# Grouped attention in a two-layer backbone: inverse sums spread by transfers through DRAM, and the bias table built one stage earlier

## What is computed

```
h = rms_norm(x, norm_g) * (1 + scale) + shift          # 1280 tokens, latent and context
q, k, v, g = split(h @ w_in)                           # 8 heads of q, 2 of k and v, 128 wide; g is 1024 wide
q, k = rope(rms_norm(q, q_g)), rope(rms_norm(k, k_g))  # rope on the latent tokens alone
s = q @ k.T * 128 ** -0.5                              # latent q: 1280 keys; context q: 256 keys
o = softmax(s) @ v                                     # = (exp(s - max) @ v) / sum(exp(s - max))
y = (o * silu(g)) @ w_out
```

## Time and profile before

| | |
|---|---|
| median of 3 runs | 1547.32 us (1546.25 to 1550.59) |
| profiled execution | 1546.84 us, its span 1545.1 us |
| TensorE | 1495.9 us busy, 97% of the span |
| VectorE | 1003.6 us, 65% |
| ScalarE | 811.1 us, 52% |
| GpSimd | 419.4 us, 27% |
| DMA | 252.23 MB; SP's queue 51.5% of 16 engines' span |
| mean granted TensorE clock | 0.988 |

### The profile page before, as it was taken

The page is one execution under the profiler, slowest core; times in us unless marked ns, Lnnn a source line. Parts: engine busy times, 40 slices in busy tenths (PEclk is TensorE's granted clock), DMA queues, the critical chain, the costliest instruction groups (busy, mean ns, idle before and its releaser), DMA issues. The chain is left out here.

```text
span 1545.1 us, 26314 instructions
## 1 busy us (share of the span) xinstructions
PE 1495.9 (97%) x9467; PEld 1310.5 (85%) x9467; DVE 1003.6 (65%) x2139; ACT 811.1 (52%) x1848; POOL 419.4 (27%) x513
## 2 busy tenths in 40 slices
PE   6999999999999999989999999999998999999998
PEld 3788788897898898978888888889997889899996
DVE  5665645428888888864348966576221887787883
ACT  7422321128777777754554333444111887777772
POOL 2322101002222111100012333221390454554541
PEclk9899999999999999999999999999998999999999
DMA  9435425409111244023224454478957999999882
GB/s 358 161 122 157 129 83 178 159 18 274 24 25 24 81 157 143 7 88 116 82 89 127 131 166 139 132 219 268 288 142 216 301 297 272 257 264 274 260 232 68
DMA packets 195653, 252.23 MB, mean 163 GB/s; under 512 B 32978, under 2 KB 157476, under 8 KB 195492
## 3 DMA queue, kind: packets, MB, share of 16 engines
q1 hardware_dynamic: 193076, 242.16, 51.5%
q10 hardware_dynamic: 2448, 8.39, 1.9%
HBM read 187.59 MB, written 78.76 MB: 172 GB/s over the span
## 5 line engine op out<-in xcount | busy, mean ns | idle before, releaser
L1195 ACT ACTIVATE prob<-S,nm,qk_inv 128x512 f32<-128x512 f32 (+1 forms) x208 | 146.3, 707 | 3.5 <-DVE nm L1131 3.5
L600 PE MATMUL pp<-h_hi,w_hi 128*128 128x512 f32 (+1 forms) x408 | 147.6, 362 | 0.0
L2593 DVE CUSTOM_DVE_ANT_0 nprob<-nS,bias_set 128x640 f32<-128x640 f32 x128 | 105.0, 821 | 61.6 <-PE nS L2425 40.5
L601 PE MATMUL pp<-h_lo,w_hi 128*128 128x512 f32 (+1 forms) x408 | 144.6, 354 | 0.0
L602 PE MATMUL pp<-h_hi,w_lo 128*128 128x512 f32 (+1 forms) x408 | 144.5, 354 | 0.0
L2511 ACT CAST npt_hi<-nTB 128x256 fp32r<-128x256 f32 (+1 forms) x256 | 103.7, 425 | 61.2 <-PE nTB L2436 54.5
L1149 DVE TENSOR_TENSOR ptlo<-TB,pthi 128x512 fp32r<-128x512 f32 (+1 forms) x192 | 114.5, 596 | 29.8 <-ACT pthi L1207 28.0
L1207 ACT CAST pthi<-TB 128x512 fp32r<-128x512 f32 (+1 forms) x192 | 99.3, 517 | 63.1 <-PE TB L1076 62.4
L1124 DVE TENSOR_REDUCE mx<-S 128x1 f32<-128x512 f32 (+1 forms) x208 | 116.5, 579 | 10.7 <-PE S L1068 9.4
L2608 DVE TENSOR_TENSOR npt_lo<-nTB,npt_hi 128x256 fp32r<-128x256 f32 (+1 forms) x256 | 115.2, 482 | 2.8 <-ACT npt_hi L2511 1.5
L2502 ACT ACTIVATE nprob<-nprob,selector 128x640 f32<-128x640 f32 x128 | 106.5, 832 | 10.7 <-DVE selector L2593 10.0
(11 more groups left out here) (328 smaller groups left out, 4481.2 us busy)
## 6 DMA issues: line engine op xcount, KB each, us to landing
kq_scratch<-p_stage SPq DMA_DIRECT2D x96, 256.0 KB, 3.9
keys<-kq_scratch SPq DMA_DIRECT2D x32, 768.0 KB, 5.1
bias_set<-bias_scratch SPq DMA_DIRECT2D x64, 384.0 KB, 6.3
v_strip<-v_scratch SPq DMA_DIRECT2D x128, 128.0 KB, 5.2
wearly<-in_mod_w SPq DMA_DIRECT2D x15, 1024.0 KB, 7.5
bias_scratch<-bias_wide_scratch SPq DMA_DIRECT2D x16, 768.0 KB, 10.8
w_raw<-in_na_w_in SPq DMA_DIRECT2D x11, 1024.0 KB, 6.0
wside<-in_mod_w SPq DMA_DIRECT2D x9, 1024.0 KB, 7.2
```

The source lines that it names most:

```text
L600: pe.matmul(acc, whi[:, k, ws], hi[:, k, a:a + width], start=(k == 0), stop=False)
L601: pe.matmul(acc, whi[:, k, ws], lo[:, k, a:a + width], start=False, stop=False)
L1195: act.activation(prob[:, p % 5, a:a + n], S[:, score_bank(p, k), 0:n], ACT.Exp, bias=nm[:, p % 5:p % 5 + 1], scale=q_scale(h - 1, p) if p ...
```

## The change

It has two parts. First, the inverses of a group no longer go through PE. SP stores the two columns of `rec` (128 partitions, 8 bytes each) to a row of DRAM, `inv_row`, and loads this row into all 128 partitions of `inv`, which is now double (`n % 2`). The two transposes, their wait for `recd`, and the copy at line 1156 are gone; DVE's multiplication now waits for the load (`inv_in`) and reads every second element of `inv`. SP's list in the attention is now, for each of the 40 groups n, a store and a load, and for n = 5, 10, ... 35 also the gate load of the next head. Second, the transfers that build the bias table move to the first block. `bias_part(n)` stands at the end of SP's step n there: the middle at n = 0, three gap fills at each of n = 1 to 7 and one at n = 8, six small transfers at each of n = 1 to 8, two of the row transfers at each of n = 10 to 17. They wait for each other as before.

```diff
+                def bias_part(n):
+                    if n == 0:
+                        bias_middle(sp, io, filled)
+                        return
+                    for i in range(3 * (n - 1), min(3 * n, len(BIAS_GAPS))):
+                        bias_fill(sp, io, i, tabled)
+                    if n == 1:
+                        sp.wait_ge(filled, 16)
+                    for i in range(6 * (n - 1), min(6 * n, KINDS * STRIP_W)):
+                        bias_space(sp, io, i // STRIP_W, i % STRIP_W, spaced)
+                    if n == NQK:
+                        sp.wait_ge(spaced, 16 * KINDS * STRIP_W)
+                    for i in range(2 * (n - NQK), 2 * (n - NQK) + 2):
+                        if i >= 0:
+                            bias_rows(sp, io, *divmod(i, 8), tabled)
...
                     if n >= NQK:
                         store(n - NQK)
+                    bias_part(n)
+                sp.wait_ge(tabled, 16 * (len(BIAS_GAPS) + HALVES * 8))
...
+                def store_inverses(n):
+                    q = 2 * (n % GQA_GROUPS)
+                    sp.wait_ge(recd, n + 1)
+                    if n >= GQA_GROUPS:
+                        inverses_moved(sp, inv_in, n - GQA_GROUPS)
+                    sp.dma_start(inverse_row(n).rearrange("(p s) -> p s", s=2), rec[:, q:q + 2]).then_inc(inv_out[n % 2], 16)
+                def load_inverses(n):
+                    inverses_moved(sp, inv_out, n)
+                    if n >= 2:
+                        sp.wait_ge(od, n - 1)
+                    sp.dma_start(inv[:, n % 2, :], inverse_row(n).rearrange("(a n) -> a n", a=1).broadcast_to([P, 256])
+                                 ).then_inc(inv_in[n % 2], 16)
+                for n in range(QH * GQA_GROUPS):
+                    store_inverses(n)
+                    load_inverses(n)
+                    if n % GQA_GROUPS == 0 and n:
+                        load(n // GQA_GROUPS)
...
                         at_least(pe, lod, CHUNKS, h, chunk_no(2 * gr + 1, len(key_chunks(q)) - 1))
-                        at_least(pe, recd, GQA_GROUPS, h, gr)
                         at_least(pe, od, GQA_GROUPS, h, gr - 1)
-                        for s in range(2):
-                            pe.transpose(O[:, 256 + s * P:256 + (s + 1) * P],
-                                         rec[:, q - 1 + s:q + s].broadcast_to([P, P]), consts["ident"][:, :])
...
+                    if GQA_GROUPS * h + gr >= GQA_GROUPS:
+                        inverses_moved(dve, inv_out, GQA_GROUPS * (h - 1) + gr)
                     dve.reciprocal(rec[:, q:q + 2], tot[:, q:q + 2]).then_inc(recd, 1)
...
-                    dve.tensor_copy(inv[:, :], O[:, 256:512]).then_inc(invd, 1)
-                    at_least(dve, invd, GQA_GROUPS, h, gr)
-                    dve.tensor_tensor(qk[:, bass.ds(head, 1), tok:tok + 256].rearrange("p a n -> p (a n)"),
-                                      O[:, 0:256], inv[:, :], ALU.mult).then_inc(od, 1)
+                    n = GQA_GROUPS * h + gr
+                    inverses_moved(dve, inv_in, n)
+                    dve.tensor_tensor(qk[:, bass.ds(head, 1), tok:tok + 256].rearrange("p a (s n) -> p (a s) n", s=2),
+                                      O[:, 0:256].rearrange("p (s n) -> p s n", s=2),
+                                      inv[:, n % 2, :].rearrange("p (n s) -> p s n", s=2), ALU.mult).then_inc(od, 1)
```

More of the change, by code:

```diff
@@ L465, in norm_and_first_projections @@
         vw_hi, vw_lo, vmm = c.sem("vw_hi"), c.sem("vw_lo"), c.sem("vmm")
+        filled, spaced, tabled = c.sem("bias_filled"), c.sem("bias_spaced"), c.sem("bias_tabled")
         v_hi, v_lo, q0h, q0l = c.sem("v_hi"), c.sem("v_lo"), c.sem("q0_hi"), c.sem("q0_lo")
@@ L884, in bias_gaps, with bias_middle, bias_fill, bias_space @@
     return [(a, b) for a, b in ((0, v0), (v0 + KH * KEY_W, LOCAL)) if a < b]
-BIAS_FILLS = sum(len(bias_gaps(f, r)) for f in range(HALVES) for r in range(8))
 def bias_place(io):
     return io["bias_table"].rearrange("h k (r c) f n -> (h k) f r c n", c=STRIP_W)
-def bias_fill(sp, io, filled, tabled):
+def bias_middle(sp, io, filled):
     sp.dma_start(io["bias_wide"].rearrange("h k c e w -> (h k c) (e w)"), io["mask_mid"]).then_inc(filled, 16)
[L898 to L904, removed]
-    shift = (0, -8, -16)[kind]
[L907 to L913, removed]
-    taps = io["bias_wide"].rearrange("h k c e w -> (h k) c (e w)")
[L916 to L920, removed]
+BIAS_GAPS = [(f, r, a, b) for f in range(HALVES) for r in range(8) for a, b in bias_gaps(f, r)]
+def bias_fill(sp, io, n, tabled):
+    f, r, a, b = BIAS_GAPS[n]
+    sp.dma_start(bias_place(io)[:, f, r, :, a:b], io["mask_cols"][:, :, 0:b - a]).then_inc(tabled, 16)
+def bias_space(sp, io, kind, c, spaced):
+    shift = (0, -8, -16)[kind]
+    k0 = (max(c - 8, 0), c, min(8 + c, 16))[kind]
+    at = k0 + shift - c + GRID_W - 1
+    sp.dma_start(io["bias_wide"][:, kind, c, :, k0:k0 + KW], io["bias"][:, :, at:at + KW]).then_inc(spaced, 16)
+def bias_rows(sp, io, f, r, tabled):
+    taps = io["bias_wide"].rearrange("h k c e w -> (h k) c (e w)")
+    v0 = first_key_row(f, r)
+    e0 = v0 + 4 * f - (8 * f + r) + KH - 1
+    sp.dma_start(bias_place(io)[:, f, r, :, v0 * KEY_W:(v0 + KH) * KEY_W],
+                 taps[:, :, e0 * KEY_W:(e0 + KH) * KEY_W]).then_inc(tabled, 16)
 GQA_TILES = [(NCTX + P * j, T) for j in range(NLAT // P)] + [(P * j, NCTX) for j in range(CT)]
@@ L985, in grouped_attention @@
         g = c.sb("gate_in", [P, T])
-        inv = c.sb("inv_sums", [P, 256])
+        inv = c.sb("inv_sums", [P, 2, 256])
         mx, sums = c.sb("mx", [P, 5, 3]), c.sb("sums", [P, GQA_N, 3])
@@ L993, in grouped_attention @@
         topd = c.sem("g_max_raw")
-        totd, recd, gated, invd = c.sem("g_total"), c.sem("g_recip"), c.sem("g_gated"), c.sem("g_inv")
+        totd, recd, gated = c.sem("g_total"), c.sem("g_recip"), c.sem("g_gated")
+        inv_out, inv_in = ([c.sem(f"g_inv_{x}{i}") for i in range(2)] for x in ("stored", "loaded"))
         td, hid, lod = c.sem("g_turned"), c.sem("g_pt_hi"), c.sem("g_pt_lo")
         pvd, od, gl = c.sem("g_pv"), c.sem("g_out"), c.sem("g_gate_in")
-        filled, spaced, tabled = c.sem("bias_filled"), c.sem("bias_spaced"), c.sem("bias_tabled")
         def pt(p):
@@ L1014, in live, with inverse_row, inverses_moved @@
             return (n >= 0 or prev) and not (tail and n >= 0)
+        def inverse_row(n):
+            return io["inv_row"][n % GQA_GROUPS]
+        def inverses_moved(eng, sems, n):
+            eng.wait_ge(sems[n % 2], 16 * (n // 2 + 1))
         def q_scale(h, p):
@@ L2761, in backbone @@
         io["gd"] = scratch("gate_scratch", [KT, P, T])
+        io["inv_row"] = scratch("inv_scratch", [GQA_GROUPS, 2 * P])
         io["kq"] = scratch("kq_scratch", [PAIRS, STRIPS, P, KQ_IN])
```

## The result

The changed kernel takes 1572.94 us, the median of 4 runs (1571.61 to 1573.84), against 1548.95 (1546.25 to 1550.97) for the kernel before in 4 runs: a ratio of 1.0157 with a 95% interval of 1.0141 to 1.0172. I had said 1554, range 1544 to 1568. The direction was right, the size was not: the time lies above the range.

What follows compares the result with a forecast made beforehand. TensorE, busy for 97% of the span, was taken as the bound. From 1546.84 us, - 12 (attention) + 14.8 (four stops) + 4.3 (gate tile) = + 7.1 gave 1553.9, stated as 1554 us, range 1544 to 1568.

Steps and rivals of the forecast that it cites:

- The stops: First projections: weights issued 6.7 us later against 3.03 us of slack stop TensorE in tiles 3, 5, 7, 9; 14.8 us.
- The gate tile's stop: First block, step 11: two row transfers ahead of tile 14's weights, 4.6 us against 0.36 us of slack; a 4.3 us stop.
- The clock: First block: TensorE's granted clock was to stay at 1.00 in the stops, so nothing was added for it.
- rival 3: First block: the clock falls to half speed after each of five stops, 3 us each, 15 us; 1569 us, chance 0.12.
- The attention: Attention without transposes and copy: 12 us less; wrong if it gave more than 15 us or less than 8.
- The transposes: Attention, TensorE: removing two per group, 0.21 us by their starts, gives 7.8 us.
- the copy and the `od` waits: Attention: without the 0.41 us copy ten `od` waits shrink, 4.1 us, and the last group ends earlier, 0.4 us.
- the last pair: Last group's inverse store and load: 6.0 us of room for 5.2 to 8.0 us; cost 0 to 2.6 us, taken as 0.
- the stride of two: VectorE's multiplication reads every second element of `inv`: between 0 and double its 0.42 us, taken as 0.
- the traffic that left the attention: Attention: 87 DMAs and their traffic leave it; this gives nothing.
- the odd steps' transfers: First projections: at odd steps they delay only `beside.load`, whose buffer is used a step later; no stop in even tiles.
- Rival 1: First block: nine transfers issue in under 3.03 us, 0.34 us each, so the weights are not late enough; 1535 us, chance 0.13.

Runs made afterwards that it cites:

- experiment 4: Changed kernel with 9, 6, 3 and 0 bias transfers ahead of the weights load at steps 1, 3, 5, 7, the rest ahead of the next swap: 1561.53 us, one run.
- experiment 3: Changed kernel plus 18 spare matmuls on TensorE ahead of `add_squares` in tiles 3, 5, 7 and 9: 1569.37 us, ratio 1.013 to the kernel before.
- experiment 6: Changed kernel with `bias_part` moved ahead of `swap`, plus the 80 transposes again, unused, on constant data: 1549.17 us, ratio 0.9999 to the kernel before.
- experiment 7: Changed kernel with `bias_part` moved ahead of `swap`, plus VectorE's copy of 256 columns again, unused: 1545.73 us, ratio 0.9979 to the kernel before.
- experiment 8: Changed kernel with `bias_part` moved ahead of `swap`, and the last two groups' inverses by TensorE's transposes and VectorE's copy: 1540.14 us, ratio 0.9941 to the kernel before.
- experiment 1: Changed kernel with the inverses by TensorE's transposes as before, the table still in the first block: 1580.94 us, ratio 1.0201 to the kernel before.
- experiment 5: Changed kernel with the table's transfers back in the attention, behind each group's inverse load: 1584.55 us, ratio 1.0219 to the kernel before.

## Why the prediction was wrong in size

**The stops** were right in cause, place and number: squares, behind the weights, behind `bias_part`, in tiles 3, 5, 7 and 9. 14.8 us were predicted, 17.6 measured. The slack of 3.03 us held: at step 1 the weights came 7.5 us late (93.73, then 101.23) and PE stopped for 4.4. The issue was 6.24, 7.61, 6.0 and 6.3 us for the predicted 6.7. The miss of 0.7 us per stop is the weights' landing, 5.7 to 6.5 us where it had been 5.3. With fewer transfers ahead it was 6.4 and 8.2 us for three and 5.2 for none (experiment 4, the last of the second trace). I had weighed data on their way for the rows and not for the fills; that it is the fills' data which delay the load fits these numbers, but no run separates it.

**The gate tile's stop** was 3.4 us for 4.3, and at another place than I said: PE does not wait for tile 14's weights but one step earlier, inside `beside.turn`, for ScalarE's `beside.take`, which stands behind `high(14)` and the gate. The chain is the one I named, with another last link. The weights came 3.7 us late for my 4.6: 2.8 us by the issue of the two rows, which I had put at 1.3, and 0.9 by the landing.

**The clock is the step that failed.** The forecast had it at 1.00 in the stops; the fall was rival 3, with a chance of 0.12. It cost 12.6 us of the 19.9 between the predicted + 7.1 and the measured + 27.0, and experiment 3 gives 10.4 of it back by filling four of the five stops. The attention below makes 6.7 of the 19.9, the stops 1.9, and the rest takes off 1.3. I had the rows that speak for it and a rule of the Trainium skill ("TensorE: Matmul & The Clock Gate", Why this matters for your kernels), which asks for no idle gaps of this length between bursts of matmuls. I set both aside because PE had stood still several times there. The trace agrees with the rule at 3.4 to 5.7 us; the stops of 2.8 and 3.0 us in the two traces of experiment 4 lost clock too, and the one of 1.9 us did not. The 1.8 us at the fifth stop are a remainder that no run filled. Rival 3 priced five stops at 3 us, 15; they cost 1.8 to 3.0 each.

**The attention** gave 5.3 us, not 12, which is outside the 8 to 15 that I had named. Two terms were too large. The transposes, 7.8 us or 0.97 per head by their starts, were worth 0.65 per head alone (experiment 6); the copy and the `od` waits, 0.51 per head predicted, were worth 0.49 alone (experiment 7), but together only 0.94. With less of its own work, PE meets ScalarE: the weight loads for the transposes of the exponentials wait longer than before. In the attention of the kernel before, then of the changed one:

```profile
PEld TB L1076 <- ACT prob L1195: 5.3, 17, 0.7
```
```profile
PEld TB L1113 <- ACT prob L1231: 8.6, 31, 0.7
```

I had allowed 0.3 us for this. That ScalarE sets part of the pace is read from these waits and from DVE's on `pthi`, 35.0 us against 28.0 before; no run took ScalarE's work away, so it isn't shown. The other term is the last pair, for which I took 0 of my 0 to 2.6: DVE waited 6.3 us in two groups, and 3.4 us of it came back in experiment 8.

**What held.** 38 of 40 pairs are hidden, though a pair takes 6.9 us of transfers and not 5.5; the stride of two costs nothing (0.415 us for 0.424); the traffic that left the attention was worth nothing (experiment 1); the odd steps' transfers are free. Rival 1 fell: issue took 0.67 us a transfer, as in the earlier trace rows, and the three fills the same, not 1.33.

## What to carry to other kernels

Before something is put into an in-order queue, find the load behind it that has the least slack: the same nine transfers cost 7 us ahead of it and nothing behind it. The issue is not the whole price, since the load may land later too: three transfers, issued in 2.06 us of a slack of 3.03, stopped PE in one of two traces. A stop of the busiest engine is to be priced with the slower work that follows it; here 1.9 us stopped cost 2.0, 2.8 cost 4.5, and 4.7 cost 7.3. When work leaves the busiest engine, ask which engine it meets next, and look at the last turn of the loop by itself, where the cover is thinner.

## What I had not expected of the hardware

A load of one 1 KB row of DRAM into 128 partitions lands after 4.0 us (3.2 to 5.2), as long as the gate's 640 KB before the change; the store of 8 bytes from each of 128 partitions takes 2.9 (2.5 to 4.7), and up to 9.8 behind a row transfer of 768 KB (experiment 5). The 40 loads of the inverses at a glance: the tile `inv_sums` of the changed kernel, us to landing,

```profile
DMA to landing us min/median/max: 3.2/4.0/5.2
```

And spare matmuls in place of a stop shorten a block: 72 of them, 17 us of work, took 10.4 us off the stretch with the four stops.
